# Eight heads at a time or four pairs of heads: regrouping four attentions of a two-block network

## The reference

```python
s = einsum('bqhd,bkhd->bhqk', q, k) * 0.125 + bias      # A, B, D, E differ in the bias
p = softmax(s, axis=-1)
out = einsum('bhqk,bkhd->bqhd', p, v)
# D: bias = rel_table[:, clip(q - k, -128, 128) + 128]
```

## Time and profile before

| what | value |
|---|---|
| median of 3 runs | 2274.04 us (2272.51 to 2276.78) |
| the profiled execution, its own time | 2286.41 us |
| its span in the profile | 2284.3 us |
| PE busy | 2208.1 us, 97% of the span |
| DVE busy | 1521.3 us, 67% |
| ACT busy | 1184.3 us, 52% |
| mean granted clock of PE | 0.989 |

### The profile page before, as it was taken

One profiled execution on the slowest core, in us unless ns is written; L12 is line 12 of the kernel. 1 busy time (PEld: TensorE's weight loads), 2 busy tenths in 40 slices (PEclk: granted clock), 3 DMA queues, 4 the chain that ended last, 5 costly groups with the idle time before them and its releaser, 6 DMA issues.

```text
span 2284.3 us, 45071 instructions
## 1 busy us (share of the span) xinstructions
PE 2208.1 (97%) x18355; PEld 2145.9 (94%) x18355; DVE 1521.3 (67%) x2344; ACT 1184.3 (52%) x1852; POOL 122.7 (5%) x146
## 2 busy tenths in 40 slices
PE   5999998899999999999999999999999999989998
PEld 5999987899999999888999999988999999989998
DVE  5766657676666666666766666677766666667664
ACT  5644453665456544446654554535654554556543
POOL 2001000110011001001100000100100000101001
PEclk9999998999999999999999999999999999999999
DMA  7555532356565657423665665642765665635653
GB/s 240 179 180 175 165 120 65 111 177 206 181 194 168 209 180 236 156 80 106 207 199 188 198 188 192 220 142 86 224 194 187 195 202 183 188 101 180 191 193 102
DMA packets 383756, 393.29 MB, mean 172 GB/s; under 512 B 6897, under 2 KB 381809, under 8 KB 383425
## 3 DMA queue, kind: packets, MB, share of 16 engines
q1 hardware_dynamic: 381632, 383.30, 52.7%
q0 software_dynamic: 1920, 7.11, 1.1%
HBM read 389.34 MB, written 1.05 MB: 171 GB/s over the span
## 4 chain that ended last, share of the span: by engine, by line
PE 86%; DVE 6%; ACT 4%; issue 2%; POOL 1%; DMA 1%; SPq 0%; POOLq 0%; DVEq 0%; ACTq 0%
PE acc L598 24%; PE acc L599 24%; PE acc L602 24%; DVE w_lo L1376 2%; ACT w_hi L984 2%; PE acc L616 2%; PE acc L617 2%; PE acc L618 2%; PE acc L567 1%; PE acc L569 1%; PE acc L568 1%; POOL t L1883 1%; PE wide L727 1%; DMA raw<-in_ffn_w_in 1%; PE wide L782 1%
## 5 line engine op out<-in xcount | busy, mean ns | idle before, releaser
L1376 DVE TENSOR_TENSOR w_lo<-raw,w_hi 128x1024 fp32r<-128x1024 f32 (+2 forms) x790 | 897.8, 1139 | 503.7 <-ACT w_hi L984 501.3
L984 ACT ACTIVATE w_hi<-raw 128x1024 fp32r<-128x1024 f32 (+2 forms) x790 | 776.3, 988 | 806.6 <-PE acc L602 739.4
L598 PE MATMUL acc<-hn_hi,w_hi 128*128 128x256 f32 x3328 | 792.7, 280 | 25.3 <-DMA colc<-in_cols 18.1
L599 PE MATMUL acc<-hn_lo,w_hi 128*128 128x256 f32 x3328 | 786.3, 278 | 0.0
L598 PEld LDWEIGHTS acc<-hn_hi,w_hi 128*128 128x128 f32 x3328 | 628.9, 189 | 30.6 <-DMA colc<-in_cols 18.1
L599 PEld LDWEIGHTS acc<-hn_lo,w_hi 128*128 128x128 f32 x3328 | 629.1, 189 | 0.9 <-issue 0.8
L602 PE MATMUL acc<-hn_hi,w_lo 128*128 128x256 f32 x3328 | 449.6, 278 | 0.0
L602 PEld LDWEIGHTS acc<-hn_hi,w_lo 128*128 128x128 f32 x3328 | 412.6, 188 | 0.0
L599 PE MATMUL acc<-hid_lo,w_hi 128*128 128x256 f32 x1408 | 331.6, 277 | 0.0
L598 PE MATMUL acc<-hid_hi,w_hi 128*128 128x256 f32 x1408 | 331.5, 277 | 0.0
L599 PEld LDWEIGHTS acc<-hid_lo,w_hi 128*128 128x128 f32 x1408 | 264.8, 188 | 0.0
(11 more groups left out here) (255 smaller groups left out, 2261.5 us busy)
## 6 DMA issues: line engine op xcount, KB each, us to landing
raw<-in_ffn_w_in SPq DMA_DIRECT2D x88, 1024.0 KB, 5.1
raw<-in_ffn_w_out SPq DMA_DIRECT2D x32, 1024.0 KB, 5.2
raw<-in_ffn_pre_w_gate SPq DMA_DIRECT2D x22, 1024.0 KB, 5.4
raw<-in_ffn_pre_w_up SPq DMA_DIRECT2D x22, 1024.0 KB, 5.3
raw<-in_ffn_post_w_gate SPq DMA_DIRECT2D x22, 1024.0 KB, 5.3
raw<-in_ffn_post_w_up SPq DMA_DIRECT2D x22, 1024.0 KB, 5.4
raw<-in_x_w_kv SPq DMA_DIRECT2D x16, 1024.0 KB, 5.5
raw<-in_ffn_pre_w_down SPq DMA_DIRECT2D x16, 1024.0 KB, 5.1
```

Of the source, the lines that this page charges most:

```text
L598: nc.tensor.matmul(bank, wh[:, j, :], a_hi[:, u.k0 + j, :], start=u.first and j == 0, stop=False)
L599: nc.tensor.matmul(bank, wh[:, j, :], a_lo[:, u.k0 + j, :], start=False, stop=False)
L984: nc.scalar.activation(w_hi[:, u.slot, 0:u.nk, :], raw[:, u.raw % RING, 0:u.nk, P * u.half:P * u.half + P], ACT.Copy).then_inc(w_hi_ready, 1)
L1376: nc.vector.tensor_tensor(w_lo[:, u.slot, 0:u.nk, :], raw[:, u.raw % RING, 0:u.nk, P * u.half:P * u.half + P], w_hi[:, u.slot, 0:u.nk, :]. ...
```

## The change

`attend` works in five steps on pairs of maps instead of eleven steps on one. In step m:

- PE takes the scores of both maps of pair m one right behind the other: their operands lie on partitions 0 to 63 and 64 to 127, so they use the two halves of the array's rows, and they go to two banks. The weighing of pair m - 1 takes both heads together too, each into 64 of the array's columns (B has one weighing of 128 columns). Units stand between: scores, first list, transposes of the one map, second list, transposes of the other, third list, weighing.
- DVE handles a pair by one bias instruction over 128x768, two maxima, one reciprocal and two products; ACT keeps its four exponents and two copies for a pair, but now in the order first list, first copy, exponents, second list, second copy, third list.
- The bias of D is laid out on the host in the order in which it is used (it depends on the distance alone), comes in two DMA issues instead of eight, and the mask is added by DVE in four instructions, two between the projections `cc` and `ch` and two after `ch`. The products with the reversed identity are gone.
- One half unit moves from ahead of the head norm into B; the number of units is unchanged.

```diff
+        def pair_of(a, m):
+            return flat(a)[:, 2 * TRI * m:2 * TRI * (m + 1)].rearrange("p (h c) -> p h c", h=2)
+        def gate_pair(m):
+            return pair_of(work[:, 8:16, :], m) if m < 2 else pair_of(keep[:, 4:8, :] if m < 3 else gates_hid, 0)
+        def both(a):
+            return a.unsqueeze(1).to_broadcast([P, 2, TRI])
+        def slot_pair(m):
+            return prob[:, :, :, :].rearrange("p a b t -> p (a b t)")[:, 2 * TRI * (m % 2):2 * TRI * (m % 2 + 1)]\
+                .rearrange("p (h c) -> p h c", h=2)
...
+            q0, k0, bias, v, out0 = {"A": (16, 20, gate_pair, vals(32, 4), 0), "B": (24, 28, lambda m: both(chunked), vals(36, 4), 4),
+                                     "D": (16, 20, band_pair, vals(36, 4), 4), "E": (28, 32, lambda m: both(dil_bias), vals(40, 4), 0)}[kind]
+            def heads(m):
+                return [(half(q0, 2 * m + j), half(k0, 2 * m + j)) for j in range(2)]
+            def values(m):
+                return [v[:, :, P * m:P * m + P]] if kind == "B" else [v[:, :, P * m + 64 * j:P * m + 64 * j + 64] for j in range(2)]
+            return heads, bias, values, out0
...
-                    att("A", spread(memk[5:8] + span("bq", "bk")))
+                    att("A", deal(memk[5:8] + span("bq", "bk"), 1, 1, 1, 1, 1, 0, 1, 1, 0, 1, 1, 0, 1, 1, 0))
...
-                    att("B", [memv[4:6], memv[6:8], [(0, 4)], half[0:1], half[1:2], half[2:3], half[3:4], [], [], [], []])
-                    head(cat[:, 4:8, :], 4, 128, ["subln"] * 4, half[4:6], half[6:8])
+                    att("B", [[memv[4:6], memv[6:8], [(0, 4)]], [half[0:1], half[1:2], []], [half[2:3], [], []],
+                              [half[3:4], [], []], [half[4:5], [], []]])
+                    head(cat[:, 4:8, :], 4, 128, ["subln"] * 4, half[5:6], half[6:8])
...
-                    project("cb", "cc", "ch")
+                    project("cb", "cc")
+                    s.band_bias(range(0, 2))
+                    project("ch")
+                    s.band_bias(range(2, 4))
                     s.conv(span("dq", "dk"))
                     c.conv += 1
                     project("dv")
                     memv, half = span("memv1"), span("mixout1a")
                     head(work[:, 16:24, :], 8, 64, ["odd"] * 4 + [("odd", 1)] * 4, memk[0:4], memk[4:8])
-                    s.band_bias(c)
-                    att("D", [memv[0:2], memv[2:4], memv[4:6], memv[6:8] + [(0, 4)], half[0:1], half[1:2], half[2:3], half[3:4],
-                              half[4:5], half[5:6], half[6:8]], final=True)
+                    att("D", [[memv[0:2], memv[2:4], []], [memv[4:6], memv[6:8], [(0, 4)]], [half[0:1], half[1:2], half[2:3]],
+                              [half[3:4], half[4:5], half[5:6]], [half[6:7], half[7:8], []]], final=True)
...
-                    att("E", spread(span("rq", "rk", "rg")), final=True)
+                    att("E", deal(span("rq", "rk", "rg"), 1, 1, 1, 1, 1, 0, 1, 1, 0, 1, 1, 0, 1, 1, 1), final=True)
...
+            def attend(c, kind, between, final):
+                heads, _, values, _ = attention(kind)
+                def score(m):
+                    if kind in "BE" and m < 2:
+                        pe.wait_ge(rot_added, c.rot - 2 + 2 * m)
+                    if m:
+                        pe.wait_ge(biased, c.att + 2 * m)
+                    for j, (q, k) in enumerate(heads(m)):
+                        nc.tensor.matmul(wide[:, j, 0:P], q[:, 0:P], k[:, 0:P], start=True, stop=True)
+                    for j, (q, k) in enumerate(heads(m)):
+                        nc.tensor.matmul(wide[:, j, P:TRI], q[:, P:T], k, start=True, stop=True).then_inc(scores, 1)
+                def turn(m, j, n):
+                    pe.wait_ge(probs, c.att + 2 * m + 2)
+                    if c.pv + n:
+                        pe.wait_ge(turned_copied, c.pv + n)
+                    p = slot_pair(m)[:, j, :]
+                    for b in range(3):
+                        mm = nc.tensor.transpose(wide[:, 2, P * b:P * b + P], p[:, P * b:P * b + P], ident)
+                    mm.then_inc(turned, 1)
+                def weigh(m):
+                    vs = values(m)
+                    n, size = len(vs) * m, P // len(vs)
+                    pe.wait_ge(turned_copied, c.pv + n + len(vs))
+                    if c.group + m:
+                        pe.wait_ge(att_out, c.group + m)
+                    o = [wide[size * j:size * j + size, 3, 0:T] for j in range(len(vs))]
+                    for j, v in enumerate(vs):
+                        nc.tensor.matmul(o[j], v[:, 0, :], slot_turned(n + j)[:, 0:T], start=True, stop=False)
+                    for j, v in enumerate(vs):
+                        nc.tensor.matmul(o[j][:, P:T], v[:, 1, :], slot_turned(n + j)[:, T:TRI], start=False, stop=True)\
+                            .then_inc(attended, 1)
...
+                for m in range(5):
+                    if m < 4:
+                        score(m)
+                    take(between[m][0])
+                    if m and kind != "B":
+                        turn(m - 1, 0, 2 * m - 2)
+                    take(between[m][1])
+                    if m and kind != "B":
+                        turn(m - 1, 1, 2 * m - 1)
+                    elif m:
+                        turn(m - 1, 1, m - 1)
+                    take(between[m][2])
+                    if m:
+                        weigh(m - 1)
...
-            def band_bias(c):
-                pe.wait_ge(band_in, 16 * 9)
-                pe.wait_ge(head_std, c.head)
-                for h in range(8):
-                    if h >= 4:
-                        pe.wait_ge(band_masked, h - 3)
-                    nc.tensor.matmul(wide[:, h % 4, 0:TRI], reverse, lower(band(h)), start=True, stop=True)\
-                        .then_inc(band_turned, 1)
-                pe.wait_ge(band_masked, 8)
...
+                def exponent(m):
+                    act.wait_ge(biased, c.att + 2 * m + 2)
+                    for j in range(2):
+                        for qt in range(2):
+                            p = slot_pair(m)[:, j, P * qt:TRI if qt else P]
+                            e = nc.scalar.activation(p, p, ACT.Exp, bias=pair_nmax[:, m % 2, j, qt:qt + 1],
+                                                     accum_out=pair_rsum[:, m % 2, j, qt:qt + 1])
+                        e.then_inc(expd, 1)
+                def copy_turned(n):
+                    act.wait_ge(turned, c.pv + n + 1)
+                    if n >= 2:
+                        act.wait_ge(attended, c.pv + n - 1)
+                    nc.scalar.activation(slot_turned(n), wide[:, 2, 0:TRI], ACT.Copy).then_inc(turned_copied, 1)
...
+                for m in range(5):
+                    take(between[m][0])
+                    if m and kind != "B":
+                        copy_turned(2 * m - 2)
+                    if m < 4:
+                        exponent(m)
+                    take(between[m][1])
+                    if m:
+                        copy_turned(per * m - 1)
+                    take(between[m][2])
+                    if m and final:
+                        act.wait_ge(att_out, c.group + m)
+                        cat_split_blocks([out0 + m - 1])
...
+                def bias(m):
+                    dve.wait_ge(scores, c.att + 2 * m + 2)
+                    if m >= 2:
+                        dve.wait_ge(turned, c.pv + per * (m - 1))
+                    p = slot_pair(m)
+                    link(nc.vector.scalar_tensor_tensor(p, wide[:, 0:2, 0:TRI], 0.125, bias_of(m), ALU.mult, ALU.add))
+                    nc.vector.tensor_reduce(pair_nmax[:, m % 2, :, 0], p[:, :, 0:P], AX.X, ALU.max, negate=True).then_inc(biased, 1)
+                    nc.vector.tensor_reduce(pair_nmax[:, m % 2, :, 1], p[:, :, P:TRI], AX.X, ALU.max, negate=True).then_inc(biased, 1)
+                def normalise(m):
+                    dve.wait_ge(expd, c.att + 2 * m + 2)
+                    p, r = slot_pair(m), pair_rinv[:, m % 2]
+                    link(nc.vector.reciprocal(r, pair_rsum[:, m % 2]))
+                    if kind != "B":
+                        for qt, cols in enumerate((slice(0, P), slice(P, TRI))):
+                            nc.vector.tensor_tensor(p[:, :, cols], p[:, :, cols],
+                                                    r[:, :, qt:qt + 1].to_broadcast([P, 2, P + P * qt]), ALU.mult).then_inc(probs, 1)
+                    else:
+                        nc.vector.tensor_scalar(rinv_lam, r[:, 1, :], neg_lam, None, ALU.mult)
+                        nc.vector.tensor_scalar(p[:, 0, 0:P], p[:, 0, 0:P], r[:, 0, 0:1], None, ALU.mult)
+                        nc.vector.tensor_scalar(p[:, 0, P:TRI], p[:, 0, P:TRI], r[:, 0, 1:2], None, ALU.mult).then_inc(probs, 1)
+                        dve.wait_ge(probs, c.att + 2 * m + 1)
+                        nc.vector.scalar_tensor_tensor(p[:, 1, 0:P], p[:, 1, 0:P], rinv_lam[:, 0:1], p[:, 0, 0:P], ALU.mult, ALU.add)
```

(55 more changed lines are left out.)

151 lines of the change are left out of this document (14 added, 137 removed).

## The result

The changed kernel takes 2254.25 us (2250.2 to 2259.4, 4 runs), the kernel before 2273.61 beside it: ratio 0.990, interval 0.9875 to 0.9926, **19.4 us faster** where 20.4 were forecast. Two later sets of runs gave 0.9903 (0.9881 to 0.9926) and 0.9904 (0.9876 to 0.9932). The ratios are the measurement's own and not quotients of the medians: in these two sets the medians differ by 21.2 and 25.7 us.

The account below looks back on a forecast made before the run. PE's own stream was taken as the bound, with 86% of what ended last. Savings of 4.2 (A), 4.4 (E), 8.1 (D) and 3.7 (B) made 20.4 us, for a median of 2253.6 us, range 2243 to 2267.

Parts of the forecast that it names:

- A pair for the price of one: On PE, paired products cost what one costs: scores save 13.6 us over 16 pairs, weighings 9.6 over 12.
- Rival 2: Column halves don't overlap in the weighings of A, D and E: 9.6 us not saved, 2263 us; chance 0.06.
- A, -4.2: Attention A: eleven units and steps of 9.73 us sum to 47.3 us against 51.5.
- E, -4.4: Attention E: twelve units and three steps of 9.9 us sum to 50.7 us against 55.1.
- D, -8.1: Attention D: 54.6 us against 62.7, including the reversal of 6.9 us that leaves PE.
- B, -3.7: Attention B: one chain of 6.5 us a step saves 6.5 us; 16 us at half clock return 2.8; bounds 6.5 and 1.5.
- The wait of 1.26 us: PE waits 1.26 us for ACT's split and copy before weighing, in all of A and three of E's four pairs.
- the 0.65 us at E's rotation: End of E: the rotation waits 0.65 us for the copy out, against 0.5 before.
- rival 1: More is gained: smaller waits in A, E and D, and B at its 6.5; 10.7 us more, some 2244; chance 0.17.
- 3: ACT and DVE follow worse: second copies slip, B and D steps lengthen; some 10 us less gained, 2264; chance 0.18.
- 5: Emptying PSUM becomes the bound: the pairs' 23.2 us return as waits and 3.8 of DVE's additions show; 2271; chance 0.04.
- 4: Slower: exponents of 1.8 us stand between ACT's split and copy in all 16 pairs, 29 us; 2282; chance 0.05.

Follow-up runs that it names:

- e2: Kernel before with only the Toeplitz band changed: two loads for eight, no reversal on PE, four additions on DVE; 2267.8 us, ratio 0.9967.
- a0: The changed kernel run again without any edit, as base of other runs; 2253.7 us, ratio 0.9903 to the kernel before.
- e6: Changed kernel with ACT copying the transposed second map ahead of the second list's split; 2254.6 us, ratio 0.9892 to the kernel before.
- f1: Changed kernel with B's units dealt more evenly among its five steps, in the same order; 2247.9 us, ratio 0.9886 to the kernel before.
- a1: The changed kernel run a third time without any edit; 2249.2 us, ratio 0.9904 to the kernel before.
- e3: Changed kernel with the scores of a pair issued head by head; 2258.6 us, ratio 0.9917 to the kernel before.
- e4: Changed kernel with the weighing of a pair issued head by head; 2257.6 us, ratio 0.9911 to the kernel before.

## Why the prediction was right

**A pair for the price of one** (scores 0.85, weighing 0.80) held to 0.01 us. Rival 2 fell. Its rule (the Trainium skill, TensorE: Matmul & The Clock Gate, Part 3, What overlaps and what doesn't: weight loads overlap with running products only when the row group differs) speaks of weight loads, and this trace shows the contrary for column halves: the second head's loads, over the same rows, lie inside the first head's products (the row of PEld above), and a pair of weighings takes 0.80 us, as one did.

By the windows: **A, -4.2:** -5.3. **E, -4.4:** -5.3 up to the rotation, then 1.7 given back by its clock: -3.6. **D, -8.1:** -9.5, of which the reversal, 6.9, is confirmed alone by e2 (6.8); steps of 15.2, 8.9, 8.4 and 6.7 us against 15.9, 9.3, 8.8 and 7.2. **B, -3.7:** -4.1, with 6.8 us at half clock inside the window where the forecast had 16. Its steps of one chain took 7.4 (in a0) to 8.5 us where 6.5 were written, or 8.3 at half clock, so a chain forecast too short and a clock forecast too low offset each other. Together 22.5 us where 20.4 were forecast and the first medians gave 19.4.

That the two totals lie within 1 us of each other is in part luck: the ratio's interval is 17 to 28 us, and B's window alone came out 5.3, 4.1 and 1.4 us shorter in three executions of the changed kernel, by the clock. What the traces bear out are the terms of A and D, which hardly varied.

The one term mis-sized in all places is the transposes: I charged 0.47 for both of a pair, from a row where the weighing came next. Where a unit comes next they take 0.25 (298.65 to 298.90 above; 963.53 to 963.78 in D; 0.30 at 1492.80 in E). Twelve such times 0.2 is 2.4 us, about the excess over the sum. The wait of 1.26 us was right to the digit in A; it stands in all four pairs of A and in three of E, as forecast, at the first pair of each with 1.5.

**The step that failed:** the 0.65 us at E's rotation. I had overlooked that DVE's low part for the last unit, with ACT's split ahead of it, stands ahead of the last copy out: 2.1 us, and in five of the ten executions that had this wait a fall of the clock that cost 1.7 more. A slip in rival 1's sum changed nothing: 10.7 us off 2253.6 is 2243, not 2244 or 2245.

**The rivals.** 1 (more gained): 2 of its 10.7 us by the windows, through the cheaper transposes, not through smaller waits. 3 (ACT and DVE follow worse): not there in A, D and E; B's longer steps are of its kind. 5 (emptying PSUM, the memory that PE writes to; the Trainium skill, TensorEngine Tiling (Array Packing), Performance Considerations, PSUM Bottleneck, says that the copies out of it may become the bound after packing) did not bind by amount: DVE's bias took 0.95 us and ACT's copies 0.47 in steps of 9.4. But ACT's copy is in the path of each weighing, with 0.6 us even when the split stands behind it (e6), and once it is hidden PE waits in D for DVE's maps, which stand behind low parts and copies alike. 4 didn't come up in the changed kernel, and did in part in f1.

## What to carry to other kernels

Here two products that use different row halves or different column halves cost what one costs, in either order; what they cost instead is how closely the other engines must follow, so read each engine's list around the short chain between two PE steps. Hiding one engine's wait paid nearly in full only where PE waited for no other engine (A) and not at all where it did (D): try such an edit place by place, keep it where the trace shows it pays, and take the clock's share off first, since one fall more or less (1.7 us in E) was as large as the yield. Match the same instructions of two traces before explaining a difference between profiled executions: some 8 of the 31.5 us here had nothing to do with the change.

## What the hardware showed that was not expected

- Products of 128 x 256 in a row started 0.113 or 0.117 to 0.118 us apart, for 100 us and more at a time, at a granted clock of 1.00 and with PE busy in both. Which of them an execution showed at 86 to 264 and at 746 to 957 us varied among executions of one kernel; from 1150 to 1440 us all fourteen had 0.113. The two stretches make 5.8 and 7.1 us, 12.9 of the 17.5 us between the profiled executions a0 and a1; single times of one kernel differ by 6 to 19 us in a set of six or more.
- Products on the two halves of the array started beside each other whatever the order of issue (e3, e4), 7 to 13 ns apart.
- In B the same kernel spent 6.8, 10.2 and 23.9 us at half clock in three executions; B took 76.7, 77.7 and 81.0 us, some 0.25 us for each microsecond at half clock.
